# A two-layer transformer pair on one core: order of the first transfers, the hybrid mixer's ScalarE hooks, and the banks of a feed-forward stage's first step

## The reference

```python
def adaln_sublayer(x, m, f, ln_g, ln_b):
    shift, scale, gate = m[:, None, 0], m[:, None, 1], m[:, None, 2]
    y = f(x * (1 + scale) + shift)
    return layer_norm(DEEPNORM_ALPHA * x + (1 + gate) * y, ln_g, ln_b)

# first_block, for each layer: cs = silu(c)
mod = (cs @ mod_w[layer] + mod_b[layer]).reshape(bsz, N_SUB, 3, D_MODEL)
# f is 0.5 * swiglu, then a mixer, then 0.5 * swiglu
def swiglu(u, w_gate, w_up, w_down):
    return (jax.nn.silu(u @ w_gate) * (u @ w_up)) @ w_down      # D_FF = 2816
```

## Time and profile before

| | us |
|---|---|
| median of 3 runs | 1635.11 |
| lowest, highest | 1632.1, 1638.12 |
| the profiled execution | 1632.25 |
| its span in the profile | 1630.4 |
| granted clock of PE, mean | 0.95 |
| busy in the span: PE, DVE, ACT | 1476.4 (91%), 1155.9 (71%), 863.9 (53%) |
| loaded from memory | 303.59 MB, 187 GB/s over the span |

### The profile page before, as it was taken

How to read it: one execution, slowest core, us unless ns; L and a number is a source line. 1 busy time by engine, 2 the same in 40 slices (tenths; PEclk the granted TensorE clock), 3 DMA queues, 4 the chain that set the end, 5 groups by cost and what they waited for, 6 DMA issues and landing times. The chain is left out here.

```text
span 1630.4 us, 23366 instructions
## 1 busy us (share of the span) xinstructions
PE 1476.4 (91%) x8807; PEld 1263.8 (78%) x8807; DVE 1155.9 (71%) x2075; ACT 863.9 (53%) x1581; POOL 0.2 (0%) x4
## 2 busy tenths in 40 slices
PE   3999999986978999989999898899997997799987
PEld 2888879876857888878887795788886994699745
DVE  5988878958658888798887666886666435644364
ACT  1544544561446455465444557555546946575463
POOL 0000000000000000000000000000000000000000
PEclk9999999998979999999999899999998998899887
DMA  9999767630034898658886061575556440546000
GB/s 368 319 315 336 275 221 252 210 112 9 1 104 177 297 322 302 205 201 302 307 299 223 26 227 40 180 267 198 188 190 191 138 160 30 152 113 226 1 1 26
DMA packets 197236, 306.13 MB, mean 188 GB/s; under 512 B 10535, under 2 KB 158854, under 8 KB 197126
## 3 DMA queue, kind: packets, MB, share of 16 engines
q1 hardware_dynamic: 195456, 303.23, 54.6%
q10 hardware_dynamic: 1670, 1.43, 0.3%
HBM read 303.59 MB, written 1.05 MB: 187 GB/s over the span
## 5 line engine op out<-in xcount | busy, mean ns | idle before, releaser
L927 PE MATMUL bank<-u_hi_lo,w_hi 128*128 128x512 f32 x1344 | 473.9, 397 | 12.1 <-DVE arena L989 12.1
L926 PE MATMUL bank<-u_hi_lo,w_lo 128*128 128x256 f32 x1176 | 328.6, 279 | 0.0
L978 DVE TENSOR_TENSOR w_lo<-weight_ring,w_hi 128x1024 fp32r<-128x1024 f32 x264 | 307.7, 1219 | 11.5 <-ACT w_hi L948 10.8
L927 PEld LDWEIGHTS bank<-u_hi_lo,w_hi 128*128 128x128 f32 x1344 | 246.8, 188 | 63.7 <-DVE arena L989 15.0
L948 ACT CAST w_hi<-weight_ring 128x1024 fp32r<-128x1024 f32 x264 | 260.3, 1047 | 8.4 <-DMA weight_ring<-in_ffn_w_up_dram 5.2
L926 PEld LDWEIGHTS bank<-u_hi_lo,w_lo 128*128 128x128 f32 x1176 | 222.5, 189 | 7.4
L1167 DVE TENSOR_TENSOR wp_lo<-weight_ring,wp_hi 128x1024 fp32r<-128x1024 f32 (+4 forms) x149 | 167.4, 1162 | 53.3 <-ACT wp_hi L1134 53.0
L849 PE MATMUL bank<-src_hi,wp_hi 128*128 128x256 f32 (+2 forms) x672 | 194.0, 302 | 0.9 <-ACT src_hi L435 0.5
L849 PE MATMUL bank<-src_hi,wp_lo 128*128 128x256 f32 (+2 forms) x672 | 182.3, 286 | 0.0
L849 PE MATMUL bank<-src_lo,wp_hi 128*128 128x256 f32 (+2 forms) x672 | 182.2, 286 | 0.0
L1134 ACT CAST wp_hi<-weight_ring 128x1024 fp32r<-128x1024 f32 (+4 forms) x149 | 143.8, 1008 | 62.5 <-PE bank L849 56.3
(11 more groups left out here) (358 smaller groups left out, 2186.8 us busy)
## 6 DMA issues: line engine op xcount, KB each, us to landing
weight_ring<-in_mod_w_dram SPq DMA_DIRECT2D x72, 1024.0 KB, 6.9
weight_ring<-in_ffn_w_gate_dram SPq DMA_DIRECT2D x44, 1024.0 KB, 5.8
weight_ring<-in_ffn_w_up_dram SPq DMA_DIRECT2D x44, 1024.0 KB, 5.5
weight_ring<-in_ffn_w_down_dram SPq DMA_DIRECT2D x44, 1024.0 KB, 8.3
weight_ring<-in_hyb_w_in_dram SPq DMA_DIRECT2D x16, 1024.0 KB, 8.0
weight_ring<-in_w_in_e_dram SPq DMA_DIRECT2D x16, 1024.0 KB, 5.8
weight_ring<-in_w_in_o_dram SPq DMA_DIRECT2D x13, 1024.0 KB, 5.5
weight_ring<-in_hyb_w_out_dram SPq DMA_DIRECT2D x4, 1024.0 KB, 4.8
```

The source lines that it names most:

```text
L926: nc.tensor.matmul(bank[:, 0:SEQ], w[1], u[:, 0:SEQ], start=False, stop=False, skip_group_check=True)
L927: last = nc.tensor.matmul(bank[:, :], w[0], u, start=kt == 0, stop=kt == KT - 1, skip_group_check=True)
L978: nc.vector.tensor_tensor(part_view(wl, n, part), raw, part_view(wh, n, part).bitcast(F32), ALU.subtract).then_inc(w_lo.sem, w_lo.up())
```

## The change

1. **Tables.** Of the table only the 128 columns of the identity are loaded at the start by the ACT queue. The other 1844 columns (0.94 MB), pos_row, pos_col twice and phi_w2 three times leave that queue and become, with the three row vectors, the ten loads of `late_inputs()`, which SP issues before tile n = 21. DVE waits for all ten at the end of the first feed-forward stage, and in `gate_inputs`.
2. **Order of transfers.** SP issues tile 8 only when tile 3 has landed, 9 when 5 has, 10 when 7 has; x_tok goes before tile 8 instead of before tile 6.
3. **Opening.** ACT makes the fp32 numbers of chunks 2 and 3; the gate tile of step 0 is split before the columns are waited for, the up tile after chunk 1.
4. **First banks.** After a `LayerNorm` head the gate and up products of step 0 go into banks 4 and 5, so that step 1 doesn't wait for their sums. `Opening` keeps banks 0 and 1.
5. **Hybrid.** SiLUs, squares, ReLUs and norms move from `act_mid` to `act_post`, behind the eviction; SiLUs of heads 4 and 5 come earlier; sums of heads 2 and 3 come before job 14; `gate_values` goes to DVE's place 15, the scales of the heads two by two to 15 and 16. The rows of ln_g and ln_b move from the in-projection to the out-projection.

```diff
@@ the ACT queue at the start
-            for i, (dst, src) in enumerate([(tab[:, :], D["tables"])] +
+            for i, (dst, src) in enumerate([(tab[:, 0:P], D["tables"][:, 0:P])] +
...
-            for i in range(3):
-                load(phi_w2[:, i, :], D["phi_w2_2"][0, i // 2])
-            load(pos_row[:, :], D["positions"][0, :].partition_broadcast(P))
-            for a in range(TT):
-                load(pos_col[:, a:a + 1], D["positions"][0, a * P:(a + 1) * P].rearrange("(p o) -> p o", o=1))
+        def late_inputs():
+
+            pos = D["positions"][0]
+            out = [(tab[:, P:ntab], D["tables"][:, P:ntab]), (pos_row[:, :], pos.partition_broadcast(P))]
+            out += [(pos_col[:, a:a + 1], pos[a * P:(a + 1) * P].rearrange("(p o) -> p o", o=1)) for a in range(TT)]
+            out += [(phi_w2[:, i, :], D["phi_w2_2"][0, i // 2]) for i in range(3)]
+            return out + [(bc[key], src.partition_broadcast(P)) for key, src in row_vectors]
@@ Opening
-            scalar_chunks = ()
+            first_banks = (0, 1)
+            scalar_chunks = (2, 3)
...
             def act(self, act, split_hi, hi):
+                split_hi(0, 0)
                 act.wait_ge(mod_taken.sem, 2)
                 for c in range(4):
                     self.high(act, hi, c)
-                    if c == 0:
-                        split_hi(0)
+                    if c == 1:
+                        split_hi(0, 1)
+                self.floats(act)
 
             def dve(self, dve, split_lo, hi, lo):
+                split_lo(0, 0)
                 dve.wait_ge(mod_done.sem, 2)
                 for u in range(2):
                     mod_take(dve, u)
                 for c in range(4):
                     self.low(dve, hi, lo, c)
-                    if c == 0:
-                        split_lo(0)
+                    if c == 1:
+                        split_lo(0, 1)
@@ LayerNorm
-            scalar_chunks = (2, 3)
+            first_banks = (4, 5)
@@ ffn
+            def gate_up_bank(j, part):
+
+                return PB[part if j else head.first_banks[part]]
...
+                if not m:
+                    dve.wait_ge(inputs_in, 16 * len(late_inputs()))
                 dve.drain().then_inc(stage_done.sem, stage_done.up())
...
-                        if part < 2:
+                        if part < 2 and (j > 1 or head.first_banks[part] == part):
                             summed = up_summed if part else gate_summed
                             pe.wait_ge(summed.sem, summed.base + j)
@@ hybrid
-            pe_pre = {3: turn_small, 9: pe_steps(sum_of=0), 10: pe_steps(0, 1), 11: pe_steps(1), 12: pe_steps(2, 2),
-                      13: pe_steps(3, 3), 16: decays_ahead}
-            act_mid = {4: take_small, 7: act_steps(silus=[0]), 8: act_steps(silus=[1]), 9: act_steps(silus=[2]),
-                       10: act_steps(0, silus=[3]), 11: act_steps(1, tables=True, gates=True, root_of=0),
-                       12: act_steps(2, root_of=1), 13: act_steps(3, root_of=2), 14: act_steps(root_of=3),
-                       15: act_steps(silus=[4, 5], tables=True)}
-            dve_at = {6: gate_inputs, 12: dve_steps(0), 13: dve_steps(1, gates=True, scale=0), 14: dve_steps(2, scale=1),
-                      15: dve_steps(3, scale=2), 16: dve_steps(scale=3, cands=True), 17: dve_steps(rounds=2),
+            pe_pre = {3: turn_small, 9: pe_steps(sums=[0]), 10: pe_steps(0, [1]), 11: pe_steps(1), 12: pe_steps(2),
+                      13: pe_steps(3), 14: pe_steps(sums=[2, 3]), 16: decays_ahead}
+            act_mid = {4: take_small}
+            act_post = {7: act_steps([0]), 8: act_steps([1]), 9: act_steps([2], 0), 10: act_steps([3], 1),
+                        11: act_steps([4], 2), 12: act_steps([5], 3, True, [0, 1]), 13: act_steps(roots=[2, 3])}
+            dve_at = {6: gate_inputs, 12: dve_steps(0), 13: dve_steps(1), 14: dve_steps(2),
+                      15: dve_steps(3, True, [0, 1]), 16: dve_steps(scales=[2, 3], cands=True), 17: dve_steps(rounds=2),
                       18: dve_steps(rounds=2)}
-            projections(jobs, uT, post=post, slots=4, n_units=1, head=head, x_rows_of=(0, 3), pe_pre=pe_pre,
-                        act_mid=act_mid, dve_at=dve_at)
+            projections(jobs, uT, post=post, slots=4, n_units=1, head=head, pe_pre=pe_pre, act_mid=act_mid,
+                        act_post=act_post, dve_at=dve_at)
...
-            out_proj(w_out, mixT, 0)
+            out_proj(w_out, mixT, 0, x_rows_of=(0, 1))
@@ SP
+            ahead = {8: 3, 9: 5, 10: 7}
             for n, tile in enumerate(plan):
                 if n == 3 * RING:
-                    for key, src in row_vectors:
-                        sp.dma_start(bc[key], src.partition_broadcast(P)).then_inc(inputs_in, 16)
+                    for dst, src in late_inputs():
+                        sp.dma_start(dst, src).then_inc(inputs_in, 16)
                 if n >= RING:
                     sp.wait_ge(*plan[n - RING].freed)
-                if n == RING - 1:
+                if n in ahead:
+                    sp.wait_ge(loaded[plan[ahead[n]].slot], plan[ahead[n]].need)
+                if n == len(first_mods):
                     sp.dma_start(x_tok, D["x"].rearrange("b (a p) d -> p (b a) d", p=P)).then_inc(x_in, 16)
```

50 lines of the change are left out of this document (23 added, 27 removed).

## The result

The changed kernel takes 1611.28 us (median of 4 runs, 1609.92 to 1615.09), the kernel before in the same comparison 1634.39 (1632.10 to 1638.12). The ratio is 0.986 with an interval of 0.9835 to 0.9886: about 23 us, or 1.4%, faster.

A forecast was written before the change was run, and what follows sets the result against it. TensorE is busy for 91% of the span, so time is gained where it stands still or runs at half clock after. Hybrid 12.0 + stages 3.9 - stage 0 4.7 = 11.2 us: 1621.0 profiled, 1624 as median, range 1614 to 1633.

The forecast's parts named there:

- Opening: Start of the kernel: columns come at 34.7 instead of 37.43, and step 1 of feed-forward stage 0 starts 4.8 us earlier.
- Late loads: Stage 0: ten loads ahead of the down tile take 16.7 us, so the stage ends 4.7 us slower than before.
- Rival A: Stage 0: late loads cost little beyond their bytes, 4.5 us of the opening are kept, 1615 us in all; 20%.
- my chain: Stage 0: down tile lands at 85.9, ACT is stuck in its cast, and step 5 starts at 88.5 instead of 86.76.
- Hybrid, hooks: In-projection: with Relus and Silus behind the evictions, four PE waits (8.0 us) and 2.6 us of half clock go, 10.6 in all.
- rival C: Hybrid: hooks don't free PE, as ACT or Relu 1 comes too late; two waits staying means 6 us missing, 1630; 8%.
- Hybrid, rows of ln_g and ln_b: In-projection: moving these rows out removes the 1.37 us wait at 271.46; nothing is lost in the out-projection.
- Stages: Step 1 of the feed-forward stages at 500, 700 and 1042: PE no longer waits for the bank, 3.9 us gained together.
- Sum: Whole kernel: 12.0 + 3.9 - 4.7 = 11.2 us gained, 1621.0 profiled, 1624 as median.
- The range: Whole kernel: 1614 to 1633 us.

The follow-up runs named there:

- e4: Kernel before with only the opening and the order of transfers changed (table split, late loads, SP's waits, x_tok, ScalarE's chunks, gate split): 1627.86 us, ratio 0.9974.
- e13: Changed kernel with only the two 16-byte rows (row_a_log, row_dt_bias) before tile 21, the other late loads before tile 63: 1610.58 us.
- e18: Repeat of the changed kernel with all ten late loads before tile 63: 1610.24 us, ratio 0.986.
- e2: Kernel before with only the rows of ln_g and ln_b moved from the in-projection to the out-projection: 1629.15 us, ratio 0.997.
- e16: Kernel before with 5 matmuls of ones put in front of the hybrid's modulation reduction, where PE waits: 1632.19 us, ratio 1.0002.
- e1: Kernel before with only the hybrid's part (hooks behind evictions, rows of ln_g and ln_b moved to the out-projection): 1613.85 us, ratio 0.9879.
- e5: Changed kernel with the three row vectors first among the ten late loads: 1611.50 us, median of two.
- e7: Changed kernel with all ten late loads moved from before tile 21 to before tile 63: 1609.80 us.
- e17: The changed kernel once more, unaltered, in the same rounds as its variant with late loads before tile 63: 1612.34 us, ratio 0.9872.

## Why the prediction was wrong, step by step

**Opening: mechanism right, the size a matter of the execution.** x landed where I had put it. I carried over the 3.58 us of the reduction from a row in which PE had idled 4.54 us before it; behind the turning of x it took 1.84 in the profiled execution, but 3.41 in e4, e13 and e18. Where it stayed slow, step 1 came 4.8 to 5.4 us earlier, which is my 4.8 or little more; where it was fast from its start, 6.9 to 7.4. My sum had one of the outcomes and no term for the others.

**Late loads: the step that failed.** "For the six further small ones (positions three times, phi_w2 three times) I take the same 1.6." The price was right for the three whose price I had (4.8) and wrong for the six: 3.7 together, not 9.6. The table cost 3.4, not 2.3, and in the group of ten another 2.9 us vanish. So the block cost 8.7 us where I had 16.7. Rival A, with 0.3 each, makes the block 8.9 us, and gave the down tile's landing to half a microsecond. I gave it 20%, though the nearest rows for the six were their own, on the ACT queue. They were the same loads on another queue, and I took other loads on the same queue. Of my chain the down tile was late and ACT stood in front of its cast, but step 5 was not late: the wait came at steps 6 and 7 (1.11 and 1.59 us), behind the tiles that follow. That is also where rival A was wrong. It asked only whether the down tile's chain ends before PE needs it, kept all but 0.3 us of the opening, and 3.3 were lost. The block took 3.3 us instead of 9.5, since the first part of any such block is free.

**The Trainium skill's rule** (DMA: Bandwidth & Descriptors, "Issuing engines are not separate DMA queues"), which I set aside, pointed to the better side: by it the six loads would cost alike on either queue. Measured on SP's they cost 0.6 each, well below the 1.6 that I used. The 0.3 us that I had read on ACT's is the delay of a tile and not the price of a load, so the two can't be set side by side. No run here prices the same group on both queues, and the rule isn't shown beyond that.

**Hybrid, hooks: right.** The gain was 11.4 us against 10.6; all four waits went, the clock was at 1.00, and rival C fell (PE shows no wait at the dots).

**Hybrid, rows of ln_g and ln_b: mis-sized by 3.3.** I counted the wait of 1.37 us and not what stands in the rows behind it. The earlier trace rows has the reduction at 2.43 us, and the products behind it ran at 0.41 instead of 0.28. I had counted the half clock for the hooks, and should have looked for it behind every wait that goes. Moving the rows alone (e2) gained 4.67 us there, and filling the wait (e16) 3.35.

**Stages: right.** The gain was 3.7 us against 3.9; the wait at step 2 was 1.34, I had said about 1.1.

**Sum.** 7.4 - 4.3 + 4.5 + 11.4 - 1.0 + 3.7 - 4.2 = 17.5, against 11.2. The 1.0 and 4.2 us that came back are the clock in unchanged code. They are missing from my range, which had no term for it. The medians give 23.1; the 5.6 us more are in the main the distance of the two profiled executions from their medians, and no trace shows where they lie.

**The range.** It cut off the lower end of rival A (1615, reached down to 1614), and A's price of the block came together with gains that no rival held: 3.3 us of half clock behind the wait of 1.37, and 2.6 in the opening. The profiled execution, 1615.09, lies inside the range and the median 2.7 us below it, so what put the result outside is also the choice of one profile of before, 2.9 us under its median, as the base, and the assumption that the changed kernel would lie as far from its own.

## What to carry to other kernels

When a wait of the matrix engine goes, read the durations of the rows behind it as well: what they are above their usual length goes too, at best. Price a transfer that is moved by its own rows in its old place, before using those of its new neighbours, and find from the ring how much delay is free. A gain of a few microseconds that comes from the clock can be seen in its place in the trace and still be absent from the whole time, so judge small edits by place and take the whole time for large ones only.

## What the runs showed of the hardware

- A load of 128 rows of 16 bytes cost the queue behind it 1.6 us; one of the positions and phi_w2 (rows of 4 and 256 bytes, one load with 1 KB) 0.6 on average; one of 128 rows of 1 KB 1.3 when alone; and 0.94 MB in rows of 7.4 KB 3.4, where 1 MB tiles take 2.6. The prices add, within some tenths, in groups of up to seven, and make 3 to 4 us less than that in the group of ten. Each group but the three rows and the ten stands on one trace.
- After a standstill of 1.17 us PE kept its full clock (e4), after 1.24 and 1.37 in the same place it ran at half clock up to about 279.6 in before, some 7 us (0.41 instead of 0.28 us a product). Filled with matmuls, the same place kept the full clock twice.
- After 6.4 to 6.5 us of standing still, the same two groups of 16 matmuls in the opening took 3.28 and 1.84 us in one execution and 3.68 and 3.41 in others (e4, e13, e18), with the same code.
- Half clock taken from one place came back in others, with no change of code there: of the 3.35 us gained in e16 at 280 us, 2.0 were lost by 344 and 1.5 more at 509. Of the 4.2 us that the changed kernel lost in the unchanged attention near 1380 us, e1 and e5 lost 0 and 0.8, e7, e17 and e18 all 4.2.
